# Adding adaLN weight tiles on GpSimd: four operations of 512 columns in place of one of 2048

## The chip, the cores and the metric

The kernel runs on one core of a Trainium2 chip. The metric is the device time of one execution in microseconds (us). The kernel before was timed three times.

## What is computed

One layer of a streaming encoder block on an input of 256 tokens by 2048 features, all in float32. The part that the change touches is the modulation: `mod = c @ w_ada + b_ada`, a vector of 2048 features times a matrix of 2048 rows and 12288 columns, which gives six vectors of 2048 (shift, scale and gate for each half of the layer). Around it:

```
h = rmsnorm(x, g_mix) * (1 + sc1) + sh1
proj = h @ w_in                      # 2048 x 5376
ya = sliding-window attention of 16 heads (ALiBi, sinks) * beta_attn
yr = silu(gr) * group_norm(retention of 4 heads)
x = x + gt1 * (concat(ya, yr) @ w_out)
h2 = rmsnorm(x, g_ffn) * (1 + sc2) + sh2
x = x + gt2 * (square(relu(h2 @ w1)) @ w2)       # d_ff 8192
out = rmsnorm(x, g_final)
```

## The kernel before, in words

Weights come in groups of 1 MB. The SP queue loads a group into one of four stage buffers; ScalarE (ACT) rounds its 128x2048 floats into `w_hi` (line 519); VectorE (DVE) takes the remainder `w_lo = stage - w_hi` (`split_group`, line 1083); TensorE (PE) then multiplies with both parts (`half_feature_group`, lines 789 to 791; `feature_group`, lines 801 and 802; `token_group`, lines 815 to 817). `w_hi` and `w_lo` have two buffers each. The order of the jobs is written out by hand in `JOBS`: `w_in` in two halves, `w_out`, and then a loop of four blocks of `w1` and `w2` (the MLP).

Between its `w_lo` operations VectorE does the rest of the layer in a fixed order. Behind the second half of `w_in` it has the attention of eight pairs of heads: `logits` (lines 1116 to 1137), `normalise` (lines 1141 to 1148) and `attention_tail` (line 1156). Later come the retention's gate and group norm (lines 1161 to 1206), and for each strip of `w_out` the product with the gate and the residual add (`gated_strip`, lines 1224 and 1228; `add_residual`, lines 1236 to 1241).

The modulation is computed without the big matrix product. A tile is 128 rows of `w_ada` by 2048 columns, 1 MB. Each tile is multiplied by its piece of `c`, one value for each partition, and the 16 tiles of a vector are added up in `acc`; PE then sums over the partitions. The first two vectors (32 tiles) are done by VectorE (line 1030), since all else waits for them. The other four (64 tiles) are `POOL_UNITS`: SP loads the tile into one of up to four slots (`ada`, `ada_y`, and a part of `x_sb`), once the add before it in that slot has counted up `ada_used` (line 346); ScalarE scales it in place (`scale_tile`, line 562) and counts up `ada_scaled`; GpSimd (POOL) waits for that, adds the tile to `acc` (line 470), counts up `ada_used`, and waits for its own count before it goes on. `ada_loads` and `ada_before` fix at which weight group each tile is loaded and scaled: some four tiles to three groups until 48 are done, and 16 in the MLP. Loads of tiles and of weight groups stand in one SP queue in a fixed order, and ScalarE's scaling stands in one order with its rounding.

At the very end GpSimd does two pieces of 512 columns of the last product (line 482) beside VectorE, which does six (line 1410).

The lines that the text speaks of: 338 and 347 (SP's loads), 470 (the add), 519, 562, 1083, 1136, 1137, 1141, 1148, 1202, 1224, 1228, 1239, 1241.

Of the kernel before, what the change touches and what calls it, by code (L numbers as in the profile page):

```python
# [1 line left out]

# [8 lines left out]
ALU = mybir.AluOpType  # L35
# [19 lines left out]
TOK_COLS = 512  # L55
# [78 lines left out]
def build(nc, x, c, w_ada, b_ada, g_mix, w_in, beta_attn, sinks, g_ret, w_out, g_ffn, w1, w2,  # L134
          g_final, consts, decay_in, out):
    with ExitStack() as ctx:
# [3 lines left out]
        def region(kib):  # L140

            at = place["at"]
            place["at"] += int(kib * 1024)
            return at

        def sb(name, shape, dt, offset):
            return nc.alloc_sbuf_tensor_at(name, shape, dt, offset=offset)

        def sem(name):
# [16 lines left out]
        acc = sb("acc", [P, 2, D], F32, region(16))  # L166
# [58 lines left out]
        acc_zeroed, ada_scaled, ada_used, ones_set, act_scaled = map(  # L225
            sem, ("acc_zeroed", "ada_scaled", "ada_used", "ones_set", "act_scaled"))
# [49 lines left out]
        def result_of(j):  # L276

            kind, c0, _, _ = JOBS[j]
            if c0 == KV0:
                return k_dup[:, :, :]  # L280
            if c0 < KV0:
                return q_T[:, c0 // P:c0 // P + 2, :]
            if kind == "feat":
                return qk_ret[:, (c0 - QR0) // P:(c0 - QR0) // P + 2, :]
            if c0 < GR0:
                return v_ret[:, (c0 - VR0) // TOK_COLS, :, :]
            return gate[:, :, c0 - GR0:c0 - GR0 + TOK_COLS]
# [12 lines left out]
        ada_slots = [ada[:, 0, :], ada[:, 1, :], ada_y[:, :], x_sb[:, 1, :]]  # L300

        def ada_slot(n):

            if n < ADA_4:
                return (0, 1, 3)[n] if n < ADA_AHEAD else (0, 1, 3, 2)[(n - ADA_AHEAD) % 4]
            return (n - ADA_4) % 3 if n < ADA_3 else (n - ADA_3) % 2
# [122 lines left out]
        @block.gpsimd  # L429
        def _(pool):  # L430
            zeroed, biased = 0, [0, 0]

            def load_bias(dst, col, a):

                pool.dma_start(dst, b_ada[0:1, col:col + dst.shape[1]]).then_inc(bias_loaded[a], 16)
                biased[a] += 1

            def zero(a):

                nonlocal zeroed  # L440
                nc.gpsimd.memset(acc[:, a, :], 0.0).then_inc(acc_zeroed, 1)
                zeroed += 1
                pool.wait_ge(acc_zeroed, zeroed)

            for a in range(2):

                zero(a)
                load_bias(acc[0:1, a, 0:D // 2], SH1 + a * (D // 2), a)
                load_bias(acc[0:1, a, D // 2:D], SC1 + a * (D // 2), a)
            nc.gpsimd.memset(ones[:, :], 1.0).then_inc(ones_set, 1)  # L450

            def start_sum(u):

                col, a = POOL_UNITS[u]
                if col == GT2:
                    pool.wait_ge(gate_spread, STRIPS)
                else:
                    pool.wait_ge(mod_summed, u + 1)
                zero(a)
                load_bias(acc[0:1, a, :], col, a)  # L460

            start_sum(0)
            for u, (col, a) in enumerate(POOL_UNITS):
                if col == GT2:
                    start_sum(u)
                pool.wait_ge(bias_loaded[a], 32 + 16 * (u // 2 + 1))
                for k in range(KT):
                    n = u * KT + k
                    pool.wait_ge(ada_scaled, n + 1)
                    nc.gpsimd.tensor_tensor(acc[:, a, :], ada_slots[ada_slot(n)], acc[:, a, :], ALU.add).then_inc(ada_used, 1)  # L470
                    pool.wait_ge(ada_used, n + 1)
                    if n in (KT // 2, KT + KT // 2):
                        start_sum(u + 1)
                    if n == 3 * KT + 3:
                        pool.wait_ge(squares, 2 + 2 * STRIPS)
                        nc.gpsimd.memset(f_acc[:, :, :], 0.0).then_inc(f_zeroed, 1)

            pool.wait_ge(gfin_loaded, 16)
            for i, (t, n) in enumerate(POOL_PIECES):
                cols = slice(n * TOK_COLS, (n + 1) * TOK_COLS)  # L480
                pool.wait_ge(act_scaled, i + 1)
                nc.gpsimd.tensor_tensor(x_sb[:, t, cols], x_sb[:, t, cols], acc[:, 0, cols], ALU.mult).then_inc(pool_out, 1)
# [265 lines left out]
        def _(pe):  # L748
# [151 lines left out]

            for j in range(J_MLP):
                kind, _, k0, _ = JOBS[j]
                for q in range(N_GROUPS[j]):
                    g = FIRST[j] + q
# [546 lines left out]
```

## Time and profile before

| what | value |
|---|---|
| three runs | 1311.75, 1315.55, 1317.11 us; median 1315.55 |
| profiled execution, span from first to last instruction | 1309.6 us |
| PE busy | 1158.2 us, 88% |
| VectorE busy | 894.8 us, 68% |
| ScalarE busy | 591.8 us, 45% |
| GpSimd busy | 361.5 us, 28% |
| DMA | 303.74 MB, mean 232 GB/s |

The page gives the profiled execution's span alone; its whole device time beside it isn't shown, and the median of the runs lies 5.95 us above the span. An engine is counted as busy from the start of an instruction to its end, whatever it waits for inside; so a duration far over the shortest of the same shape is a wait that no row of idle time shows.

### The profile page before, as it was taken

Reading aid. Unit: us, or ns where it says so; the run is one execution under the profiler, and the core shown is the slowest. Engines: PE = TensorE matmul, PEld = TensorE weight load, DVE = VectorE, ACT = ScalarE, POOL = GpSimd, SP = SyncE. Lnnn points to the kernel's source line nnn. Section 1 sums busy time; section 2 is a strip of 40 time slices with the busy share of each in tenths; the row PEclk is TensorE's granted clock in tenths of the full one; section 3 lists DMA queues with packets and bytes.
Section 4 is the critical chain, followed back from the end, with each engine's and each line's share of the span. In section 5 each row is a group of like instructions: output and inputs, shape, how many; then the busy total and the mean of one; then the engine's idle time right before and its main releaser. Section 6 shows DMA issues by size and latency. Waiting matters only on the chain.

```text
span 1309.6 us, 15597 instructions
## 1 busy us (share of the span) xinstructions
PE 1158.2 (88%) x6163; PEld 989.2 (76%) x6163; DVE 894.8 (68%) x647; ACT 591.8 (45%) x519; POOL 361.5 (28%) x86
## 2 busy tenths in 40 slices
PE   0498999779877886899999999999999999999995
PEld 0498889568766665687878888878888788888884
DVE  5878766999899988865555555555555554555665
ACT  2244446555764555365444334534344443444342
POOL 1012207867789567233012100112000121000001
PEclk9689999788997987889999999999999999999998
DMA  9998988876677667627666666766666666665551
GB/s 372 400 347 278 314 319 296 284 249 235 250 247 265 239 233 266 193 82 240 224 236 215 195 190 187 246 214 222 188 192 220 233 220 192 192 184 183 180 192 64
DMA packets 165163, 303.74 MB, mean 232 GB/s; under 512 B 5120, under 2 KB 97920, under 8 KB 156416
## 3 DMA queue, kind: packets, MB, share of 16 engines
q1 hardware_dynamic: 164176, 300.70, 66.9%
q10 hardware_dynamic: 688, 2.40, 0.5%
q8 instruction: 29, 0.48, 0.2%
q14 instruction: 14, 0.11, 0.0%
q0 software_dynamic: 256, 0.05, 0.0%
HBM read 301.03 MB, written 2.10 MB: 231 GB/s over the span
## 4 chain that ended last, share of the span: by engine, by line
PE 63%; DVE 25%; ACT 5%; DMA 3%; issue 3%; SPq 0%; DVEq 0%; ACTq 0%
PE ps_job L801 17%; DVE w_lo L1083 12%; PE ps_job L815 9%; PE ps_job L817 9%; PE ps_job L816 9%; PE ps_job L802 9%; ACT w_hi L519 4%; PE ps_job L789 2%; PE ps_job L790 2%; PE ps_job L791 2%; DVE acc L1030 2%; DMA stage<-in_w_ada 2%; PE ps L775 2%; DVE probs_even L1148 1%; DVE gate L1202 1%
## 5 line engine op out<-in xcount | busy, mean ns | idle before, releaser
L1083 DVE TENSOR_TENSOR w_lo<-stage,w_hi 128x2048 fp32r<-128x2048 f32 x186 | 497.2, 2673 | 293.5 <-ACT w_hi L519 293.3
L519 ACT ACTIVATE w_hi<-stage 128x2048 fp32r<-128x2048 f32 x186 | 356.2, 1915 | 462.4 <-PE ps_job L817 276.5
L470 POOL TENSOR_TENSOR acc<-ada,acc 128x2048 f32<-128x2048 f32 x43 | 225.1, 5236 | 623.8 <-ACT ada L562 622.6
L801 PE MATMUL ps_job<-act_hl,w_hi 128*128 128x512 f32 x1024 | 362.3, 399 | 3.2 <-DVE w_lo L1083 3.2
L802 PE MATMUL ps_job<-act_hl,w_lo 128*128 128x256 f32 x1024 | 287.8, 281 | 0.0
L801 PEld LDWEIGHTS ps_job<-act_hl,w_hi 128*128 128x128 f32 x1024 | 192.9, 188 | 50.7 <-issue 2.8
L815 PE MATMUL ps_job<-w_hi,hid_hl 128*128 128x512 f32 x512 | 202.4, 395 | 4.5 <-DVE w_lo L1083 3.7
L816 PE MATMUL ps_job<-w_lo,hid_hl 128*128 128x512 f32 x512 | 199.5, 390 | 0.0
L817 PE MATMUL ps_job<-w_hi,hid_hl 128*128 128x512 f32 x512 | 199.4, 389 | 0.0
L802 PEld LDWEIGHTS ps_job<-act_hl,w_lo 128*128 128x128 f32 x1024 | 194.1, 190 | 0.1
L815 PE MATMUL ps_job<-w_hi,act_hl 128*128 128x512 f32 x256 | 111.0, 434 | 38.3 <-DVE w_lo L1083 38.3
L789 PE MATMUL ps_job<-act_hl,w_hi 128*128 128x256 f32 x416 | 122.5, 295 | 19.7 <-DVE w_lo L1083 12.4
L790 PE MATMUL ps_job<-act_hl,w_hi 128*128 128x256 f32 x416 | 120.8, 290 | 0.0
L791 PE MATMUL ps_job<-act_hl,w_lo 128*128 128x256 f32 x416 | 120.6, 290 | 0.0
L815 PEld LDWEIGHTS ps_job<-w_hi,hid_hl 128*128 128x128 f32 x512 | 96.1, 188 | 30.2 <-DVE w_lo L1083 9.6
L816 PEld LDWEIGHTS ps_job<-w_lo,hid_hl 128*128 128x128 f32 x512 | 96.1, 188 | 20.4 <-issue 1.0
L817 PEld LDWEIGHTS ps_job<-w_hi,hid_hl 128*128 128x128 f32 x512 | 96.1, 188 | 20.3
L816 PE MATMUL ps_job<-w_lo,act_hl 128*128 128x512 f32 x256 | 106.7, 417 | 0.0
L817 PE MATMUL ps_job<-w_hi,act_hl 128*128 128x512 f32 x256 | 106.2, 415 | 0.0
L789 PEld LDWEIGHTS ps_job<-act_hl,w_hi 128*128 128x128 f32 x416 | 83.1, 200 | 23.3 <-DVE w_lo L1083 13.1
L815 PEld LDWEIGHTS ps_job<-w_hi,act_hl 128*128 128x128 f32 x256 | 52.5, 205 | 55.2 <-DVE w_lo L1083 42.6
L562 ACT ACTIVATE ada<-ada,small 128x2048 f32<-128x2048 f32 x43 | 85.8, 2001 | 2.1 <-DMA ada<-in_w_ada 2.1
(153 smaller groups left out, 1171.9 us busy)
## 6 DMA issues: line engine op xcount, KB each, us to landing
stage<-in_w SPq DMA_DIRECT2D x128, 1024.0 KB, 5.4
ada<-in_w_ada SPq DMA_DIRECT2D x43, 1024.0 KB, 6.9
stage<-in_w_in SPq DMA_DIRECT2D x42, 1024.0 KB, 7.1
stage<-in_w_ada SPq DMA_DIRECT2D x32, 1024.0 KB, 7.0
stage<-in_w_out SPq DMA_DIRECT2D x16, 1024.0 KB, 7.2
ada_y<-in_w_ada SPq DMA_DIRECT2D x12, 1024.0 KB, 5.4
x_sb<-in_w_ada SPq DMA_DIRECT2D x9, 1024.0 KB, 5.0
x_sb<-in_x ACTq DMA_DIRECT2D x1, 2048.0 KB, 14.5
```

What stands on the lines that cost most here:

```text
L470: nc.gpsimd.tensor_tensor(acc[:, a, :], ada_slots[ada_slot(n)], acc[:, a, :], ALU.add).then_inc(ada_used, 1)
L519: nc.scalar.activation(w_hi[:, ring, :], stage[:, slot, :], ACT.Copy).then_inc(hi_ready, 1)
L562: nc.scalar.activation(ada_slots[slot], ada_slots[slot], ACT.Copy, scale=vec_T[:, bass.ds(V_C + k, 1)]).then_inc(ada_scaled, 1)
L789: nc.tensor.matmul(o, w_hi[:, ring, ws], act_hl[:, k0 + k, 0:T], start=(k == 0), stop=False)
L790: nc.tensor.matmul(o, w_hi[:, ring, ws], act_hl[:, k0 + k, T:2 * T], start=False, stop=False)
L791: last = nc.tensor.matmul(o, w_lo[:, ring, ws], act_hl[:, k0 + k, 0:T], start=False, stop=(k == 7))
L801: nc.tensor.matmul(o, w_hi[:, ring, ws], act_hl[:, kt, :], start=(kt == 0), stop=False)
L802: last = nc.tensor.matmul(o[:, T:2 * T], w_lo[:, ring, ws], act_hl[:, kt, 0:T], start=False, stop=last_group and k == 7)
L815: nc.tensor.matmul(o, a_hi, wh, start=first_group and k == 0, stop=False)
L816: nc.tensor.matmul(o, a_hi, wl, start=False, stop=False)
L817: last = nc.tensor.matmul(o, a_lo, wh, start=False, stop=last_group and k == 3)
L1083: nc.vector.tensor_tensor(w_lo[:, ring, :], stage[:, slot, :], w_hi[:, ring, :].bitcast(F32), ALU.subtract).then_inc(lo_ready, 1)
```

## The change

In the loop over the tiles, the one `tensor_tensor` of 2048 columns becomes four of 512 (`TOK_COLS` is 512), one behind the other with no wait between them. Only the last counts up `ada_used`. The same elements are added, in the same order of tiles.

```diff
                 for k in range(KT):
                     n = u * KT + k
                     pool.wait_ge(ada_scaled, n + 1)
-                    nc.gpsimd.tensor_tensor(acc[:, a, :], ada_slots[ada_slot(n)], acc[:, a, :], ALU.add).then_inc(ada_used, 1)
+                    for piece in range(4):
+                        cols = slice(piece * TOK_COLS, (piece + 1) * TOK_COLS)
+                        last = nc.gpsimd.tensor_tensor(acc[:, a, cols], ada_slots[ada_slot(n)][:, cols], acc[:, a, cols], ALU.add)
+                    last.then_inc(ada_used, 1)
                     pool.wait_ge(ada_used, n + 1)
```

## Rows read from the trace of the kernel before

**Rows 1.** Busy time of each engine in stretches; then PEclk, DMA share, GB/s.
```profile
60.00:200.00 140.00, 126.31 (x869) 118.79 (x869) 103.14 (x60) 58.51 (x44) 22.06 (x5) 0.93 0.91 320
200.00:430.00 230.00, 190.98 (x1138) 164.67 (x1138) 213.90 (x174) 133.65 (x157) 177.11 (x36) 0.88 0.74 261
430.00:560.00 130.00, 99.61 (x421) 79.58 (x421) 112.01 (x103) 65.00 (x59) 71.12 (x15) 0.87 0.63 223
665.00:765.00 100.00, 98.50 (x447) 80.72 (x446) 53.26 (x24) 42.00 (x25) 19.30 (x4) 1.00 0.62 207
765.00:845.00 80.00, 80.00 (x452) 69.32 (x451) 46.80 (x37) 34.73 (x29) 0.00 (x0) 1.00 0.67 213
```
**Rows 2.** Lines 1083 and 470 over the span: durations ns, min/median/max.
```profile
L1083 DVE TENSOR_TENSOR w_lo<-stage,w_hi x186: 2276/2293/7002, 55.9 to 1285.3; 128x2048 fp32r<-128x2048 f32 x186
L470 POOL TENSOR_TENSOR acc<-ada,acc x43: 4493/4768/7342, 92.1 to 1094.8; 128x2048 f32<-128x2048 f32 x43
```
**Rows 3.** Timeline, 272 to 286 us: start, duration, instruction.
```profile
272.10 14.03 DVE L1148 TENSOR_SCALAR probs_even<-probs_even,small 128x128 f32<-128x128 f32 x4
272.08 4.62 POOL L470 TENSOR_TENSOR acc<-x_sb,acc 128x2048 f32<-128x2048 f32 x1 [4.26 <-ACT x_sb L562]
...
281.48 4.49 POOL L470 TENSOR_TENSOR acc<-ada,acc 128x2048 f32<-128x2048 f32 x1
```
**Rows 4.** Timeline, VectorE and GpSimd at 227 and 255 us.
```profile
227.41 6.67 DVE L1083 TENSOR_TENSOR w_lo<-stage,w_hi 128x2048 fp32r<-128x2048 f32 x1
227.35 11.17 POOL L470 TENSOR_TENSOR acc<-ada,acc 128x2048 f32<-128x2048 f32 x2
255.08 1.01 DVE L1148 TENSOR_SCALAR probs_odd<-probs_odd,small 128x128 f32<-128x128 f32 x4
```
**Rows 5.** Groups of VectorE by line, 200 to 430 us.
```profile
L1083 DVE TENSOR_TENSOR w_lo<-stage,w_hi 128x2048 fp32r<-128x2048 f32 x24 | 92.9, 3872 | 18.3 <-ACT w_hi L519 18.1
L1148 DVE TENSOR_SCALAR probs_even<-probs_even,small 128x128 f32<-128x128 f32 (+1 forms) x16 | 23.7, 1715 | 0.1
L1148 DVE TENSOR_SCALAR probs_odd<-probs_odd,small 128x128 f32<-128x128 f32 (+1 forms) x16 | 17.2, 1136 | 0.1
L1136 DVE SCALAR_TENSOR_TENSOR small<-small 128x4 f32<-128x4 f32 x8 | 12.6, 1570 | 0.3
L1141 DVE TENSOR_TENSOR small<-small 128x4 f32<-128x4 f32 x8 | 11.7, 1466 | 0.0
```
**Rows 6.** Waits, 200 to 430 us: total, times, longest.
```profile
PE ps_job L815 <- DVE w_lo L1083: 16.0, 5, 5.4
PE ps_job L789 <- DVE w_lo L1083: 8.9, 1, 8.9
SPq L347 <- POOL acc L470: 157.2, 28, 14.3
```
**Rows 7.** Groups of VectorE by line, 430 to 560 us.
```profile
L1202 DVE TENSOR_SCALAR gate<-gate,small 128x256 f32<-128x256 f32 x8 | 17.5, 2231 | 0.1
L1224 DVE TENSOR_TENSOR y_part<-y_part,tmp 128x512 f32<-128x512 f32 x8 | 12.8, 1639 | 0.0
```
**Rows 8.** Waits of PE: 430 to 560 us; then 565 to 665 us.
```profile
PE ps_job L815 <- DVE w_lo L1083: 19.4, 4, 11.0
...
PE ps_job L801 <- DVE w_lo L1083: 3.2, 2, 2.5
```
**Rows 9.** Group of line 1083, 90 to 200 us.
```profile
L1083 DVE TENSOR_TENSOR w_lo<-stage,w_hi 128x2048 fp32r<-128x2048 f32 x17 | 48.7, 2864 | 25.5 <-ACT w_hi L519 25.5
```
**Rows 10.** The last products, two engines; line 482's durations; a VectorE operation of 512 columns.
```profile
1299.16 6.08 DVE L1410 SCALAR_TENSOR_TENSOR x_sb<-x_sb,small,acc 128x512 f32<-128x512 f32 x6
...
L482 POOL TENSOR_TENSOR x_sb<-x_sb,acc x2: 1647/1677/1707, 1300.1 to 1301.7; 128x512 f32<-128x512 f32 x2
...
508.68 0.68 DVE L1239 TENSOR_TENSOR x_sb<-x_sb,y_part 128x512 f32<-128x512 f32 x1
```
**Rows 11.** The page's group of line 562, with the idle time before it.
```profile
L562 ACT ACTIVATE ada<-ada,small 128x2048 f32<-128x2048 f32 x43 | 85.8, 2001 | 2.1 <-DMA ada<-in_w_ada 2.1
```

## The prediction, made before the changed kernel was run

> **What bounds the kernel now.** I read the page's busy times first, then the busy time by stretches, then the groups, the waits and the timeline of the stretches in which GpSimd adds.
>
> By stretches [rows 1] the kernel has two halves. In the MLP (665 us on) PE is busy 98.5 of 100 us in a stretch with four GpSimd adds and 80.00 of 80 us in one without any: PE bounds it, and an add costs it something. Between 200 and 560 us PE is busy for 291 of 360 us at a granted clock of 0.88 and 0.87, while VectorE is busy for 326. There VectorE sets the pace, and the waits say how PE meets it: it waits for `w_lo` [rows 6, 8].
>
> But VectorE's busy time is not work. The `w_lo` operation takes 2.29 us in the median and 7.00 at most [rows 2]. Four short products of line 1148 take 1.01 us in one place and 14.03 in another [rows 3, 4], and in the second place three GpSimd adds ran back to back from 272.08 to 285.97 (the first and the last stand in the rows). Four products of 0.25 us and three whole adds of 4.6 are 14.8, or 14.0 without the first one's head start: each product was held for an add, until no add was left. In the same way the `w_lo` of 227.41 ends 2.1 us after the first of two adds, and the second of these two takes 6.6 us in place of 4.5 [rows 2, 4]. So the two engines exclude each other for the length of a whole instruction, each in turn, wherever VectorE reads two operands from SBUF or runs a product such as line 1148. The Trainium skill, "SBUF — State Buffer", section "Who interferes with whom", states this as a rule: the shared port pair is an exclusive lock, held by whoever starts first for the whole instruction. By that rule, the trace agrees: 14.03 us for four operations is three whole adds and one short rest.
>
> What this costs VectorE now: between 200 and 430 us, `w_lo` takes 92.9 us for 24, where 24 x 2.29 = 55.0 would do, an excess of 37.9. Line 1148 takes 40.9 for 32; at 1.01 for four [rows 4] that is 8.1, an excess of 32.8. Lines 1136 and 1141 take 24.3 for 16 operations that need 0.16 each, excess 21.7 [rows 5]. Together some 92 us. Between 430 and 560 us, line 1202 takes 17.5 for 8, about 0.31 each without a wait, excess 15; line 1224 takes 12.8, where 8 x 0.65 would do, excess 7.6 [rows 7]. Some 23 us in these two lines alone.
>
> **The change part by part.** It removes 64 instructions of 4.5 us (shortest 4.49 [rows 2]) and adds 256 of 512 columns.
>
> *Price of a piece.* No add of 512 columns stands in the trace; the nearest rows are GpSimd's two products of 512 columns at the end, 1.65 and 1.71 us, beside VectorE's six operations of the same size [rows 10]. VectorE's six took 6.08 us; one costs 0.60 to 0.68 by a residual add of that size, so six cost 3.7 and 2.4 was waiting, in two waits of 1.2. GpSimd's 1.65 in turn hold a wait of about 0.5 for one VectorE operation. So a piece alone is 1.15 to 1.2 us. The lower bound is 4.49 / 4 = 1.12, the upper 1.71. I take 1.17, the reading in which both engines' rows agree: an add then costs 4.7 us in place of 4.5, with 4.49 and 6.8 as ends. The skill speaks against small pieces: "GPSIMD Engine Reference", section 3.1, counts a dispatch through two software hops for each instruction beside 4497 ns for 2048 columns. From its 2.6 cycles for an element at 1.2 GHz one gets an estimate of 60 ns fixed, a piece of 1.17 us; the trace agrees with the 4497 (4.49 [rows 2]) and shows no fixed part by itself.
>
> *What a wait becomes.* A VectorE operation that now meets an add waits up to 4.5 us; it will wait up to 1.17, and half of that when it arrives at random. But it can be met more often: GpSimd's next piece is ready at once, so each of four short products in a row pays a piece. Between 200 and 430 us there are 24 `w_lo`, 32 of line 1148, 8 each of lines 1136, 1137 and 1141, and 4 of the gate: 84 operations. About 40 follow another such operation directly and pay 1.15 (46 us), 44 arrive alone and pay 0.6 (26 us); together 72, times the share of about 0.8 in which GpSimd has something to add (177 of 230 [rows 1], more once it is slowed) is 58. VectorE gains 92 - 58 = some 34 us.
>
> *The port's own limit.* In that stretch 30 adds need 30 x 4.5 = 135 us of the port, VectorE's operations that need it about 67 (55.0 of it `w_lo`). That is 202 of 230 us now, and 30 x 4.7 + 67 = 208 after. The stretch can't fall below 208, so 22 us is the most it can give, whatever VectorE gains. Near the limit, GpSimd queues: an add's latency grows from 5.4 us to 4.7 plus what VectorE puts between its pieces, some 7.
>
> *What stands behind the adds.* SP waits 157.2 us for them between 200 and 430 [rows 6], and weight loads are queued behind those waits. What covers it now is the four stage buffers: PE's waits in this stretch are for `w_lo`, none for a load. A later add eats into that cover.
>
> The terms, by what PE now waits for `w_lo` and for VectorE's other results:
> - 60 to 200 us: 17 `w_lo` take 48.7 - 17 x 2.29 = 9.8 us too long [rows 9], and three adds run there. DMA is at 0.91 [rows 1], so what VectorE gives is partly taken by loads: 3 us (0 to 6).
> - 200 to 430 us: PE waits 24.9 us for `w_lo` [rows 6] and is idle 39. VectorE gains 34, the port allows 22; the one PE wait of 8.9 us is the place at 286 us [rows 3], where 14 us become about 5. Since GpSimd's lateness gives part back, 10 us (-3 to 22).
> - 430 to 560 us: 23 us of excess are at least five waits of an add's 4.5, of which each becomes 1.2 at most, some 16 us; PE waits 19.4 us for `w_lo` here [rows 8]. Adds end before 531 us, and part of the chain is PE's and ScalarE's own. 9 us (4 to 18).
> - 560 to 665 us: PE waits once for 2.5 us for a `w_lo` [rows 8]: 2 us.
> - MLP: 12 adds in three stretches, each idle for PE of 1.5 us in 100 [rows 1]. With pieces a `w_lo` is let in at the next boundary; 3 x 1.3 = 4 us (0 to 4.5).
>
> Sum 3 + 10 + 9 + 2 + 4 = 28 us. The profiled execution has a span of 1309.6 us; its whole time isn't shown, the median of the runs is 5.95 above its span, and I take the 28 from the median: 1315.55 - 28 = 1287.5 us. The tail after 1121 us has no add and stays.
>
> **The rivals.**
> *Gain given back (17%).* VectorE's waits shrink, but in the two middle stretches tiles come late: ACT meets a tile not yet loaded and stands in order before its rounding. For it: 157 us of SP's waits and a port at 90%. Against it: ACT now waits only 2.1 us for such a load over the span [rows 11]. Then those stretches give 19 - 14 = 5 us, and the sum is 14: 1301.5 us.
>
> *No opening between pieces (11%).* The pieces come with no semaphore between them, and if GpSimd starts the next before it gives the port up, VectorE waits as long as now. For it: only adds with a wait between them are seen to let VectorE in. Against it: the two products at the end, ready back to back, each let VectorE in [rows 10], and VectorE's own operations back to back let an add in [rows 3]. Then 64 x 0.2 = 13 us more of GpSimd, nearly all hidden or paid back: 1316 to 1318, say 1316.5 us. The skill has a sentence for it: "GPSIMD Engine Reference", section 2, a core starts the next instruction as soon as its share of the last is done. No row here shows whether the port goes with it.
>
> *Dear pieces (12%), the slower side.* The port between 200 and 531 us is the place. From (230 - 67) / 120 = 1.36 us for a piece on, the demand in 200 to 430 us exceeds the stretch as it is now, and GpSimd paces it. At 1.50, 30 x 6.0 + 67 = 247, 17 us longer; in 430 to 531 us 13 x 6.0 + 34 = 112 of 101, 11 longer; less 8 us gained in the other stretches, +20: 1335.5 us. At the upper end of 1.71 it would be over +50. For it: 1.65 and 1.71 are the only rows of this size. Against it: they hold a wait, by VectorE's rows beside them.
>
> **How the numbers follow.** The forecast has 60%: 1287.5, its own range 1270 to 1302 (terms' lower and upper ends seldom fall together). To hold eight in ten I go to 1268 and 1311, which takes in the first rival and leaves out the others for the most part. 0.5% is 6.6 us, about what a measurement of this kernel can tell. Faster by more: 60% and nearly all of the 17%, less a little for the low end of the forecast, 0.76. Within 0.5%: the second rival and scraps of the others, 0.13. Slower: the third, 0.11.
>
> **What would show it.** In the changed kernel: line 470 with 256 instructions, alone 1.15 to 1.2 us, and up to 3.5 when a `w_lo` comes between; the longest `w_lo` near 3.5 in place of 7.0; four products of line 1148 at most 6 us; VectorE's busy time down by some 55 us; PE busy for nearly 100 of 100 us in the MLP. Wrong if pieces alone take over 1.36 us, if `w_lo` still shows 6 to 7 us (no opening), or if ACT waits for loads of tiles or stages (given back).

## The result, and the profile after

The changed kernel takes 1273.92 us (median of 4 runs, 1272.27 to 1275.36), the one before 1315.63 beside it; the ratio is 0.9686 with a 95% interval of 0.9669 to 0.9703. That is 41.7 us less. The forecast was 1287.5 us, 28 less. The profiled execution has a span of 1270.5 us, 39.1 less than before.

Three rows of GpSimd and VectorE: the adds from one slot (`ada_y`) over the span (minimum, median and maximum in ns), then two rows of the timeline near 276 us, where four products of `normalise` meet the adds. `w_lo` is line 1062 now, the product line 1127, the add line 448.

```profile
L448 POOL TENSOR_TENSOR acc<-ada_y,acc x48: 1259/1296/3399, 217.1 to 501.6; 128x512 f32<-128x512 f32 x48
...
276.26 5.00 DVE L1127 TENSOR_SCALAR probs_odd<-probs_odd,small 128x128 f32<-128x128 f32 x4
...
272.79 6.94 POOL L448 TENSOR_TENSOR acc<-ada_y,acc 128x512 f32<-128x512 f32 x4
```

A product that waited for a whole add each time (14.03 us for four [rows 3]) now waits for a piece each time: 5.00 us. The add in turn takes 6.94 us, since a VectorE operation comes between its pieces; alone it takes 4.98 us (below). Both engines' numbers show the hand-over at each boundary.

Next, busy time by the stretches of [rows 1] (columns as there; GpSimd is the fifth):

```profile
60.00:200.00 140.00, 131.99 (x931) 123.65 (x932) 104.85 (x63) 63.51 (x48) 44.30 (x18) 0.95 0.96 341
200.00:430.00 230.00, 198.84 (x1187) 170.85 (x1186) 192.96 (x209) 141.58 (x161) 226.82 (x137) 0.93 0.74 263
430.00:560.00 130.00, 102.16 (x482) 83.58 (x482) 95.75 (x80) 70.46 (x74) 98.36 (x55) 0.89 0.62 218
632.00:732.00 100.00, 100.00 (x459) 83.33 (x458) 50.60 (x27) 44.80 (x26) 29.19 (x16) 1.00 0.64 216
```

Between 200 and 430 us GpSimd is busy for 226.82 of 230 us. It has taken VectorE's place as the engine that sets the pace. The page's chain of the work that ended last says so, by engine (before it was PE 63%, VectorE 25%):

```profile
PE 62%; POOL 23%; DVE 5%; DMA 5%; issue 2%; ACT 2%; SPq 0%; DVEq 0%; POOLq 0%; ACTq 0%
```

Where the time went, by landmarks in both timelines (the third of each is a row of the chain). Before: the second take of the modulation, the retention's statistics, the turn of the normed rows ahead of the MLP, and the first add of two MLP blocks.

```profile
184.86 0.17 DVE L1073 COPY small<-ps 128x8 f32<-128x8 f32 x1 [1.61 <-PE ps L775]
435.56 2.74 DVE L1178 BATCH_NORM_STATS2 small<-ps 128x6 f32<-128x256 f32 x8
558.31 10.16 PE ps L765 x64
667.53 5.00 POOL L470 TENSOR_TENSOR acc<-ada,acc 128x2048 f32<-128x2048 f32 x1 [49.91 <-ACT ada L562]
847.89 4.94 POOL L470 TENSOR_TENSOR acc<-ada,acc 128x2048 f32<-128x2048 f32 x1 [108.83 <-ACT ada L562]
```

After, the same five:

```profile
177.53 0.17 DVE L1052 COPY small<-ps 128x8 f32<-128x8 f32 x1 [1.59 <-PE ps L754]
405.93 2.73 DVE L1157 BATCH_NORM_STATS2 small<-ps 128x6 f32<-128x256 f32 x8
530.56 9.45 PE ps L744 x60
636.80 7.48 POOL L448 TENSOR_TENSOR acc<-ada,acc 128x512 f32<-128x512 f32 x4 [45.83 <-ACT ada L541]
814.34 7.41 POOL L448 TENSOR_TENSOR acc<-ada,acc 128x512 f32<-128x512 f32 x4 [105.97 <-ACT ada L541]
```

The differences are 7.3, 29.6, 27.8, 30.7 and 33.6 us. So the first stretch gained 7.3, that of the attention 22.3, that of the retention and `w_out` lost 1.9, the start of the MLP gained 3.0, and each of the three MLP blocks behind it some 2.8 (the end stands at 39.1).

The line between the second and the third stretch is one of VectorE's, and GpSimd was not equally far at it: before, 35 of the 48 adds ahead of the MLP had ended at 435.56 us, after only 33 at 405.93. On GpSimd's own row, from its add at 202.60 (after: 195.40) to the end of the 48th at 530.68 (512.35), the time fell from 328.1 to 317.0 us, 11.1 less. The other 9.4 us of the two stretches came behind the last add.

### The profile page after: what moved, and what is told of

Same layout as the page of the kernel before. It is cut to its first block, busy times and chain, and to the rows that moved or that the text cites. A ratio compares the mean times of both kernels' runs of the same rounds, so it can differ in the third digit from the quotient of the medians.

```text
span 1270.5 us, 15789 instructions
## 1 busy us (share of the span) xinstructions
PE 1142.0 (90%) x6163; PEld 978.9 (77%) x6163; DVE 829.6 (65%) x647; ACT 591.6 (47%) x519; POOL 485.5 (38%) x278
## 4 chain that ended last, share of the span: by engine, by line
PE 62%; POOL 23%; DVE 5%; DMA 5%; issue 2%; ACT 2%; SPq 0%; DVEq 0%; POOLq 0%; ACTq 0%
POOL acc L448 23%; PE ps_job L780 18%; PE ps_job L794 9%; PE ps_job L795 9%; PE ps_job L796 9%; PE ps_job L781 9%; DVE acc L1009 2%; PE ps_job L768 2%; DMA stage<-in_w_ada 2%; PE ps_job L770 2%; PE ps_job L769 2%; DMA stage<-in_w_in 1%; DVE w_lo L1062 1%; ACT w_hi L498 1%; DMA ada<-in_w_ada 1%
## 5 line engine op out<-in xcount | busy, mean ns | idle before, releaser
L1062 DVE TENSOR_TENSOR w_lo<-stage,w_hi 128x2048 fp32r<-128x2048 f32 x186 | 461.7, 2482 | 319.4 <-ACT w_hi L498 314.1
L448 POOL TENSOR_TENSOR acc<-ada,acc 128x512 f32<-128x512 f32 x172 | 314.2, 1856 | 509.2 <-ACT ada L541 507.3
L794 PE MATMUL ps_job<-w_hi,act_hl 128*128 128x512 f32 x256 | 106.8, 417 | 31.8 <-DVE w_lo L1062 31.7
L768 PE MATMUL ps_job<-act_hl,w_hi 128*128 128x256 f32 x416 | 120.9, 291 | 8.5 <-DVE act_hl L1076 7.4
L769 PE MATMUL ps_job<-act_hl,w_hi 128*128 128x256 f32 x416 | 119.2, 287 | 0.0
L541 ACT ACTIVATE ada<-ada,small 128x2048 f32<-128x2048 f32 x43 | 86.0, 2004 | 43.9 <-DMA ada<-in_w_ada 43.9
L795 PE MATMUL ps_job<-w_lo,act_hl 128*128 128x512 f32 x256 | 103.2, 403 | 0.0
L796 PE MATMUL ps_job<-w_hi,act_hl 128*128 128x512 f32 x256 | 102.8, 401 | 0.0
```

Source lines behind the costliest of these rows:

```text
L448: last = nc.gpsimd.tensor_tensor(acc[:, a, cols], ada_slots[ada_slot(n)][:, cols], acc[:, a, cols], ALU.add)
L541: nc.scalar.activation(ada_slots[slot], ada_slots[slot], ACT.Copy, scale=vec_T[:, bass.ds(V_C + k, 1)]).then_inc(ada_scaled, 1)
L768: nc.tensor.matmul(o, w_hi[:, ring, ws], act_hl[:, k0 + k, 0:T], start=(k == 0), stop=False)
L769: nc.tensor.matmul(o, w_hi[:, ring, ws], act_hl[:, k0 + k, T:2 * T], start=False, stop=False)
L794: nc.tensor.matmul(o, a_hi, wh, start=first_group and k == 0, stop=False)
L795: nc.tensor.matmul(o, a_hi, wl, start=False, stop=False)
```

## The experiments

All ran in three rounds beside the kernel before (1314.2 to 1316.5 us in these sessions). The intervals are of the ratio to the kernel before. In the diffs a minus is the changed kernel; they are cut to what each kernel has different from it.

| kernel | what | median us | ratio, 95% |
|---|---|---|---|
| the change | 4 pieces | 1273.9 | 0.967 to 0.970 |
| e1_two | 2 pieces | 1288.7 | 0.978 to 0.981 |
| e8_three | 3 pieces, 4 in the MLP | 1266.1 | 0.960 to 0.966 |
| e2_eight | 8 pieces | 1299.6 | 0.987 to 0.990 |
| e3_first48 | pieces before the MLP only | 1284.2 | 0.975 to 0.980 |
| e4_last16 | pieces in the MLP only | 1303.2 | 0.989 to 0.993 |
| e5_wait | 4 pieces, a wait between | 1283.8 | 0.973 to 0.977 |
| e6_no_add | adds of 4 columns | 1194.2 | 0.906 to 0.909 |
| e7_memsets | fills for adds | 1217.6 | 0.923 to 0.927 |
| e9_quarter | 11 adds on VectorE | 1261.8 | 0.958 to 0.962 |
| e10_half | 22 adds on VectorE | 1259.9 | 0.957 to 0.962 |
| e11_quarter_three | e9 with 3 pieces | 1262.0 | 0.957 to 0.963 |
| e12_half_whole | e10 with whole adds | 1269.2 | 0.963 to 0.969 |

**How many pieces.** There are two theories. A: the port is held for a whole instruction, and GpSimd now sets the pace in the middle. B: only VectorE's waits count, so smaller is better.

```diff
-                    for piece in range(4):
-                        cols = slice(piece * TOK_COLS, (piece + 1) * TOK_COLS)
+                    for piece in range(pieces):            # 2, 8 or 3 (4 for the last 16 tiles)
+                        cols = slice(piece * D // pieces, (piece + 1) * D // pieces)
```

> Two pieces of 1024 columns in place of four of 512. Theory A (the shared port is held for one whole instruction; since the change GpSimd's row of adds paces 195 to 512 us): a w_lo waits up to 2.3 us, an add alone costs 4.65 us (4.49 and one extra piece of (4.98 - 4.49)/3 = 0.16). VectorE's waits lie between those of before and after, GpSimd's adds are shorter: about 1285 us, half of the gain or a little more. Rival B (GpSimd's pace is not what bounds now, only VectorE's waits count): VectorE's waits are double those of four pieces, 1295 us. Rival C (what helps is only that something gets in at all): 1274, as with four.

> Eight pieces of 256 columns. Theory A: an add alone costs 4.49 + 7 x 0.16 = 5.6 us, and more VectorE operations get in between; GpSimd's 42 adds between 195 and 512 us grow by 0.65 us each and more, +27 us or more there: 1300 us or above, slower than four pieces. Rival B: VectorE waits at most 0.7 us for a piece, so 1268 us, faster than four.

> Three pieces for the first 48 tiles, four for the last 16. Two pieces gave 1288.7 us with VectorE on the chain, four 1273.9 with GpSimd on it. Theory A (two bounds that cross): an add alone costs 4.8 us, 0.16 less than with four, 42 x (0.16 + a VectorE operation less in some adds) = 7 to 20 us off GpSimd's row, while VectorE's waits grow by a third; 1268 to 1276 us. Rival (VectorE's wait still counts alone): 1279, between two and four.

Measured 1288.7, 1299.6 and 1266.1 us. Eight pieces lose 26 us to four, as A has it and against B. Two pieces lie nearer to A's 1285 than to B's 1295. Three are 2 us better than the best end of A's range, and 13 better than the rival. The chain by engine, for two, three and eight pieces:

```profile
PE 64%; DVE 23%; ACT 5%; issue 4%; DMA 3%; SPq 0%; DVEq 0%; ACTq 0%
```
```profile
PE 69%; DVE 21%; issue 4%; DMA 3%; ACT 3%; SPq 0%; DVEq 0%; ACTq 0%
```
```profile
PE 64%; POOL 26%; DVE 4%; DMA 3%; ACT 1%; issue 1%; SPq 0%; DVEq 0%; POOLq 0%; ACTq 0%
```

With two and three pieces VectorE has over 20% of the chain and GpSimd none; with four and eight GpSimd has over 20% and VectorE 4 to 5%. The best count lies where the two cross. The busy times show what is traded: VectorE and GpSimd are busy for 881.8 and 406.4 us with two pieces, 829.6 and 485.5 with four, 788.6 and 533.9 with eight. What VectorE saves in waits, GpSimd pays, and more.

A piece's price is read from the shortest adds of each size out of one slot (`ada_y`): 2362 ns for 1024 columns, 1259 for 512, and for 256:

```profile
L449 POOL TENSOR_TENSOR acc<-ada_y,acc x96: 711/732/2857, 217.9 to 528.9; 128x256 f32<-128x256 f32 x96
```

From 512 to 256 columns the time falls by 548 ns, from 1024 to 512 by 1103. That is 2.15 ns for a column and, as an estimate from these sizes, about 160 ns that each instruction costs whatever its size.

**Where the gain is.**

```diff
+                    pieces = 4 if n < 3 * KT else 1        # e3; in e4 4 if n >= 3 * KT else 1
```

> Four pieces for the first 48 tiles, one operation for the last 16 (the MLP). By the stretches of the trace before and after, the MLP's part of the gain is small: three stretches with 1.5 us of idle PE each and 2.5 us at 603 us. Expected 6 us above the full change, 1280. Rival: the MLP carries a third of the gain or more: 1288.

> The other way round: four pieces for the last 16 tiles alone. Expected 6 us faster than before, 1309.5, with PE busy 100 of 100 us where the adds of the MLP stand. Rival: 1302 or less.

Measured 1284.2 and 1303.2 us. Without pieces in the MLP 10.3 us are lost, with them there alone 11.3 are gained, and some 31 belong to the stretches before. The two parts add up to the whole. My 6 us for the MLP was too low. The rivals' 14 and 12 us (1288 and 1302) were closer both times, in e4 clearly so.

**A wait between the pieces.**

```diff
+                        if piece < 3:
+                            last.then_inc(piece_done, 1)
+                            pool.wait_ge(piece_done, 3 * n + piece + 1)
```

> Four pieces, each with a wait on its own count before the next is issued (48 MB of tiles as before). The trace shows VectorE let in between pieces without a wait. Theory A: the wait adds some 0.08 us for each piece, the gap now seen between two adds, 3 x 0.08 x 42 = 10 us on GpSimd's row between 195 and 512 us, and changes nothing for VectorE: 1280 to 1284 us. Rival (pieces without a wait keep the port part of the time, and a wait would let more VectorE operations in): VectorE busy time falls by more than 10 us; the time is 1270 or less, or GpSimd's adds grow to 8 us and it is above 1290.

Measured 1283.8 us, 9.9 above the change, as A said. VectorE's busy time fell by 10.5 us (829.6 to 819.1), which is at the rival's edge; one single operation makes up 5 of it. It is this `w_lo` of the change, with the add that it met:

```profile
350.10 7.38 DVE L1062 TENSOR_TENSOR w_lo<-stage,w_hi 128x2048 fp32r<-128x2048 f32 x1
...
350.35 4.98 POOL L448 TENSOR_TENSOR acc<-x_sb,acc 128x512 f32<-128x512 f32 x4
```

All four pieces ran before it was let in: 5.09 us of waiting at one stretch. The add is the first behind a fill and a bias load. So the rival "no opening between pieces" is real, but it happened to one of 186 `w_lo` here. The traces of two other kernels have it too, each once and each at an add right behind a fill and a bias load: in e2_eight a `w_lo` of 7.98 us that began 0.25 us before its add of eight pieces (5.58 us), in e3_first48 one of 6.84 us that began 0.30 us after it. e5 does not show that a wait cures it. There the longest `w_lo` is 3.39 us, but the one beside that add began 0.44 us before it and ran its plain 2.28 us, as it did in e1, e8 and e9, where it began 0.5 to 0.8 us ahead. The cause stays open.

**What the adds cost, and by which port.** In e6 each add has 4 columns; in e7 three fills of 2048 columns stand in its place, which write the accumulator and read nothing. So both leave out the sums of four of the six modulation vectors.

```diff
-                    (four adds of 512 columns)
+                    nc.gpsimd.tensor_tensor(acc[:, a, 0:4], ada_slots[ada_slot(n)][:, 0:4], acc[:, a, 0:4], ALU.add)    # e6
+                    nc.gpsimd.memset(acc[:, a, :], 0.0)     # e7, three times, each with a wait
```

> Each tile's add is left out but for its first 4 columns (so four of the six modulation vectors are wrong); loads, scaling and all counts stay. It bounds what the adds cost in any form. Theory A: VectorE loses all its waits (about 130 us before, 45 now) and GpSimd no longer paces: 1235 to 1250 us, with PE, ScalarE and the loads as the bound between 200 and 512. Rival (after the change the adds cost nothing more): 1270.

> In place of each tile's add three fills of 2048 columns of the accumulator, each with a wait (so the four vectors are wrong): GpSimd is busy for 5.4 us per tile, 0.9 more than with one add, and writes but reads nothing. If what VectorE waits for is the port that GpSimd reads through, w_lo is never held (2.29 us throughout) while line 1127, which was seen to wait 1.4 us beside a fill at 238 us, still is: 1245 to 1262 us. Rival (any GpSimd instruction holds it): w_lo waits up to 1.8 us and the time is 1275 or more.

Measured 1194.2 and 1217.6 us, both further down than I expected. Without the adds PE bounds the kernel nearly throughout (93% of the chain). So the adds cost 121 us as whole operations and 80 as four pieces. The rows of `w_lo` in e6 and e7, and those of the short product in e7 (line 1130 there) and in e6 (line 1124):

```profile
L1059 DVE TENSOR_TENSOR w_lo<-stage,w_hi x186: 2284/2293/2295, 55.8 to 1166.0; 128x2048 fp32r<-128x2048 f32 x186
...
L1124 DVE TENSOR_SCALAR probs_odd<-probs_odd,small x16: 279/316/351, 232.9 to 322.4; 128x128 f32<-128x128 f32 x8, 128x256 f32<-128x256 f32 x8
```
```profile
L1065 DVE TENSOR_TENSOR w_lo<-stage,w_hi x186: 2271/2293/2295, 56.5 to 1192.4; 128x2048 fp32r<-128x2048 f32 x186
...
L1130 DVE TENSOR_SCALAR probs_odd<-probs_odd,small x16: 847/1807/1987, 234.7 to 332.2; 128x128 f32<-128x128 f32 x8, 128x256 f32<-128x256 f32 x8
```

In e7 GpSimd is busy for 5.56 us a tile, longer than for an add, and no `w_lo` was held: the longest of 186 took 2295 ns, as in e6. These short products were held each time, up to nearly a whole fill (1.81 us). So `w_lo`, with two operands in SBUF, shares with GpSimd only what GpSimd reads through, while the product of line 1148 (before) meets its writes as well. The Trainium skill, "SBUF — State Buffer", section "Who interferes with whom", states this split: an operation with two inputs in SBUF contends with a GpSimd instruction that reads SBUF and not with one that only writes it, while an operation in a two-port mode, which a `tensor_scalar` can enter, contends with GpSimd. By that rule e7 agrees, with 2295 and 1987 ns.

**Moving adds to VectorE.** VectorE scales and adds in one operation of 2.35 us (line 1030 before); GpSimd's pieces hold the port for 4.98 us and need ScalarE's scaling besides. In these kernels GpSimd and ScalarE skip the tiles in `VEC_ADDS`. For its other tiles before the MLP GpSimd has four pieces in e9 and e10, three in e11, and one whole add in e12.

```diff
+VEC_ADDS = [n for n in range(4, 3 * KT) if n % 4 == 3]      # e9, e11; e10, e12: n % 2 == 1
 # VectorE, one group after ScalarE would have scaled the tile (the loop over n and the lines with a and k are left out here):
+                        if n in VEC_ADDS:
+                            dve.wait_ge(ada_full[ada_slot(n)], 16 * ada_fill(n))
+                            dve.wait_ge(ada_used, n)
+                            nc.vector.scalar_tensor_tensor(out=acc[:, a, :], in0=ada_slots[ada_slot(n)], scalar=vec_T[...],
+                                                           in1=acc[:, a, :], op0=ALU.mult, op1=ALU.add).then_inc(ada_used, 1)
```

> Four pieces, and of tiles 4 to 47 every fourth (11) goes to VectorE: one operation that scales and adds (2.35 us in the trace for the first 32 tiles) one group later, in place of ScalarE's scaling and GpSimd's add. Theory A (GpSimd and the port pace 195 to 512 us): the port is held 2.35 in place of 4.98 us for each, GpSimd's row loses 11 x 7.1 us and gains the waits for VectorE's 11; 11 x (7.1 - 2.35 - 1.2) = 39 us off that row, until VectorE or PE bounds: 1250 us, range 1240 to 1262. Rival (VectorE is as tight as GpSimd, and each operation more on it costs its length): 1274 + 11 x 2.35 - a few = 1285 or more.

> The same with every second tile from 5 to 47 (22) on VectorE. Theory A: VectorE gets 22 x 2.35 = 52 us of work and becomes the bound again, GpSimd idles in between and the two take turns with a hand-over for each tile: 1250 to 1265, no better than a quarter. Rival: the port is all that counts, and 22 x 2.6 us less of it gives 1225.

> A quarter of tiles 4 to 47 on VectorE, and three pieces in place of four for GpSimd's other tiles before the MLP. Three pieces were worth 8 us where GpSimd paced; if it still does with a quarter moved, 1255 us; if VectorE has become the bound, its longer waits make it 1262 or more.

> Half of tiles 5 to 47 on VectorE, and GpSimd's other tiles before the MLP in one operation of 2048 columns, as before the change (four pieces in the MLP). It asks what the pieces themselves are worth when GpSimd holds the port half as often. Theory A (a VectorE operation waits for the rest of a whole add): some 20 adds at up to 3.3 us more of waiting for VectorE than with pieces, half of it on the path: 1280 to 1295 us. Rival (what helped was the order and the port time alone): 1260.

Measured 1261.8, 1259.9, 1262.0 and 1269.2 us. A quarter moved gives 12 us more than the change: more work on VectorE and less time, against e9's rival, though only at the upper end of my 1240 to 1262. Half gives the same within its spread. Three pieces no longer help, since GpSimd doesn't pace any more: it is busy for 238.79 of the 315 us from 195 to 510 us in e9 and for 148.59 in e10, and in e11 it has 3% of the chain and VectorE 17%. In e12, with half moved and whole adds, the loss to e10 is only 9 us, less than the 20 to 35 that I expected: the 26 whole adds that GpSimd keeps before the MLP cost that much more than in pieces. e9 to e11 beat the kernel before and the change. By the intervals none of the three beats another, nor e8_three, the change with three pieces.

## Why the prediction was right, and where it was off

**The mechanism** held: two engines share one port, and each holds it for a whole instruction. e7 shows it by taking away GpSimd's reading while it stays busy, and the number of pieces shows the grain. The size did not hold so well. The forecast of 28 us was two thirds of the 41.7 measured, and the terms below add 11.1 to reach the 39.1 of the profiled execution.

**Price of a piece.** I took 1.17 us; it is 1.26 alone, and an add takes 4.98 in place of 4.7. I said that GpSimd would pace the stretch from 1.36 us a piece on; it paces at 1.26. That sum had 30 adds between 200 and 430 us. The trace has 32: of GpSimd's 36 instructions there [rows 1] two are fills and two are bias loads. With 32 adds the limit is (230 - 67) / 128 = 1.27 us, and the measured piece stood at it.

**What a wait becomes.** VectorE's busy time was to fall by some 55 us; it fell by 65.2.

**60 to 200 us.** Forecast 3, measured 7.3. I let the loads take half of VectorE's gain, but the DMA share could still rise, from 0.91 to 0.96.

**200 to 430 us.** Forecast 10, with the port's limit at 22; measured 22.3. This is the term most mis-sized, and that it met the port's limit is luck. By the same sum with 32 adds of 4.98 us that limit is 230 - (32 x 4.98 + 67) = 4 us, not 22. VectorE gained more because it ran ahead of the adds: it ended the stretch with two adds fewer done (33 and 35, above), and these two, some 14 us at 7 us each, had to be done in the next. The late tiles that I feared did come. ScalarE's wait for tile loads, my own sign for "gain given back", rose from 2.1 us [rows 11] to 43.9 over the span:

```profile
L541 ACT ACTIVATE ada<-ada,small 128x2048 f32<-128x2048 f32 x43 | 86.0, 2004 | 43.9 <-DMA ada<-in_w_ada 43.9
```

**430 to 560 us.** Forecast 9, measured -1.9: the step that failed. I added up VectorE's waits and took 9 us of them, but in this sum I held the port's limit against the stretch before alone. My own figures for 430 to 531 us, in the rival "dear pieces", give with the measured piece 13 x 4.98 + 34 = 99 of 101 us: an estimate that leaves 2 us to gain, not 9. The adds went on until 530.7 us before and until 512.4 after, and in the changed kernel GpSimd did the 45 from 195 us on back to back. The chain runs through them (91% of it from 195 to 512 us is line 448). Behind the last one it goes by SP, which waited with a tile's load and had the next weight group queued behind it, to `w_hi`, `w_lo` and the end of the stretch:

```profile
510.51 1.84 POOL acc L448
512.37 0.34 SPq L323
512.76 7.91 DMA stage<-in_w
```

So the adds, not VectorE, set when the stretch ended. Inside it the same happens on the way: SP could not issue a tile's load sooner (451.90 us, as the add before it ended), ScalarE waited for the tile with its rounding queued behind, and VectorE's `w_lo` for that:

```profile
456.96 2.00 ACT L541 ACTIVATE ada<-ada,small 128x2048 f32<-128x2048 f32 x1 [4.77 <-DMA ada<-in_w_ada]
458.87 1.89 ACT L498 ACTIVATE w_hi<-stage 128x2048 fp32r<-128x2048 f32 x1
...
460.79 3.31 DVE L1062 TENSOR_TENSOR w_lo<-stage,w_hi 128x2048 fp32r<-128x2048 f32 x1 [12.55 <-ACT w_hi L498]
```

That is the rival "gain given back", with its mechanism; it took all of this stretch's gain. e9, which lightens GpSimd, wins 12 us. Both middle stretches together: forecast 19, measured 20.4. That the sum came out is luck, since its two terms were wrong in opposite directions.

**MLP.** Forecast 2 + 4, measured 3.0 and 3 x 2.8; e4 has 11.3 for both. I took PE's idle time, 1.5 us in 100 [rows 1]. But the ends of PE's matmuls are modelled in the profile and overlap. The waits of the weight loads from 665 to 765 us before (total, times, longest) come closer to the 2.8 that a block gained:

```profile
PEld ps_job L815 <- DVE w_lo L1083: 3.2, 4, 1.6
```

**The other rivals.** Of "no opening", my sign was a `w_lo` of 6 to 7 us; one came, of 7.38 us. The slower side, dear pieces, did not come with four. It is real as a direction: eight pieces lose 26 us to four, though they are still faster than before.

**A term that was missing.** The sum had none for TensorE's clock. Its granted clock between 200 and 430 us rose from 0.88 to 0.93, and TensorE's busy time over the span fell from 1158.2 to 1142.0 us. How much of the gain that is, no run separates.

## What to carry to other kernels

Where GpSimd and VectorE both read SBUF, look at the spread of one shape's duration (2.3 to 7.0 us here): it is waiting inside the instruction, and no idle row has it. Cutting GpSimd's instruction moves the wait from VectorE to GpSimd and adds 0.16 us a cut. So count the port's time over the whole stretch in which GpSimd works, and cut only until GpSimd begins to pace (three pieces here, not four). The other way is to hold the port less: one fused operation on VectorE of 2.35 us for 4.98 on GpSimd. For a quarter of the tiles it gave 12 us more than four pieces; against three pieces its 4 us are not clear of the noise.

## What was not expected of the hardware

- Pieces back to back on GpSimd nearly always let VectorE in, but once all four (4.98 us) went first, with `w_lo` started 0.25 us before them. With eight pieces and in e3 it happened once each, again at an add right behind a fill and a bias load.
- Fills on GpSimd, busy 5.56 us a tile, hold no two-input operation of VectorE (2295 ns at most), but hold the short products by a scalar (1807 ns in the median for 316, line 1130 of e7).
- TensorE's granted clock between 200 and 430 us rose from 0.88 to 0.93, while the engine was busy for 198.84 us of the 230 in place of 190.98; without the adds it was 0.99 between 195 and 510 us, with TensorE busy for 312.71 of 315.
